# Expert weights loaded partition-major, and eight slab places instead of six in layer 1

## The chip, the cores and the metric

One core of a Trainium2 chip runs the whole program. The metric is device time in microseconds (us) from launch to end, lower is better. The engines are PE (TensorE), DVE (VectorE), ACT (ScalarE), POOL (GpSimd) and SP (SyncE); SP issues nearly all weight loads. The core has 16 DMA engines. Two times are to be held apart: the device time of a run, and the span of the one profiled execution, which counts from its first instruction to its last.

## What is computed

A backbone of two layers over 256 context and 256 latent tokens of width 1024, all in float32. Each layer mixes tokens (neighbourhood attention and a bidirectional recurrence) and then passes them through 16 experts, of which each token uses two of one group. Layer 1 needs the latent tokens only. The part that matters here:

```python
def grouped_moe(h, w_router, router_bias, w_gate, w_up, w_down):
    t = h.reshape(-1, shp[-1])
    scores = jax.nn.sigmoid((t @ w_router).astype(jnp.float32))
    ...
    out = jnp.zeros_like(t)
    for e in range(N_EXPERTS):
        h_e = jax.nn.silu(t @ w_gate[e]) * (t @ w_up[e])
        out = out + combine[:, e:e + 1] * (h_e @ w_down[e])
    return out.reshape(shp)
```

`w_gate[e]` and `w_up[e]` are 1024 x 512, `w_down[e]` is 512 x 1024: each is 2 MiB, and an expert has three. In the products t @ w_gate[e] the sum runs over 1024 features, in h_e @ w_down[e] over 512. A sum may be taken in any order of its terms, as long as both factors use the same.

## The kernel before

**Slabs.** Each 2 MiB weight matrix is one slab of 16 KiB in each of 128 partitions. PE sums over partitions, so a slab holds k blocks: 8 for gate and up, 4 for down. The load (`flat`, L1483) is written `(k p) n -> p k n`: partition p gets rows p, p + 128, p + 256 and so on. In memory these are single rows of 512 float32 (2 KB) for gate and up, of 1024 float32 (4 KB) for down. The left factors have the matching order: feature 128 k + p of a token stands in partition p of block k.

**Layer 0** (`dealt_experts`). 512 tokens. After the second norm the tokens are turned into rows (L1020), ACT copies them out of PSUM into `hrow` (L1988) and stores them as a table in memory; the copies of the first tile stand ahead of the sigmoid of the router scores (L1982) in ACT's order. For each expert POOL gathers its 128 rows (`feed_rows`, L2298), PE turns them back (L1066), and every product is made from high and low halves: weights are split by ACT (`high`, L2015) and DVE (`slab_lo`, L2872), then the matmuls of L1077, L1080 and L1086 (gate and up) and L1105, L1110 and L1115 (down) run. Between them DVE multiplies the up product with `f_silu` into `f_acts` (L2894), and PE turns that (L1094). Six slabs are in flight, two places for each kind (`LANE`). The expert's output is stored in `expert_table` and gathered after the last expert.

**Layer 1** (`narrow_experts(2)`). 256 tokens, up to 64 for each expert. The rows stay in SBUF as `hrow_hi` (ACT, L2001) and `hrow_lo` (DVE, L2848); selection matrices (L3011) pick an expert group's tokens by matmul (`gather_cols`, L1308). Then for each expert e:

- `into_hidden`: 16 matmuls, gate (L1328) into partitions 0 to 63 and up (L1329) into 64 to 127 of one bank. They need the gate and the up slab.
- ACT makes `gated` (L2170), DVE multiplies it with the up product into `hidden` (L3036).
- meanwhile PE runs `gather_cols` for one quarter of the next group (L1308, not for e of 12 and above) and, at even e, the scatter of the pair before (L1361).
- `turn_hidden` (L1339), ACT's copy, `down` (L1350, 8 matmuls for each half) with the down slab.

**Where slabs go in layer 1.** Slabs are numbered m = 3 e + kind. Slab m goes to place m % 6: the four ring places, a fifth (A0 + 92 KB), and a sixth over `hT`. SP issues in order, each load behind one wait (L1513). The first four wait for the ring places, which the last matrices of the layer (`in` 8 to 11, `out`) held; the fifth for the last norm (`h_ready`), the sixth for `hrow_lo` (`hrow_ready`). Slab m from 6 on waits until slab m - 6 is spent: `hidden_done` for gate and up, `halves_done` for down. The loads of the layer before that, the `("in", l, s)` and `("out", l, s)` matrices, go through the same queue and the four ring places (`fill`, L1473).

```python
w = (A["w_gate"], A["w_up"], A["w_down"])
flat = [x.rearrange("l e (k p) n -> (l e) p k n", p=P) for x in w]
...
for m in range(LANES):
    if m < SLOTS:
        sp.wait_ge(*slot_spent[last_in(base + m)])
    elif m == SLOTS:
        sp.wait_ge(sem["h_ready"], 4 * KT)
    else:
        sp.wait_ge(sem["hrow_ready"], 4)
    fill_expert(m, l * N_EXPERTS + m // 3)
```

Of the kernel before, what the change touches and what calls it, by code (L numbers as in the profile page):

```python
# [65 lines left out]
def build(nc, A, out, stop=99):  # L66
# [7 lines left out]
    def fixed(name, shape, dtype=f32, offset=None):  # L74
# [129 lines left out]
    hrow_lo = fixed("hrow_lo", [P, 4, D], f32r, offset=A0 + 16 * KB)  # L204
    y_hi = fixed("y_hi", [P, 2, D], f32r, offset=A0 + 32 * KB)
# [16 lines left out]
    pick4 = fixed("pick4", [P, 4, 4 * 64], f32r, offset=A0 + 48 * KB)  # L222
    pickw4 = fixed("pickw4", [P, 4, 4 * 64], offset=A0 + 52 * KB)
    gated = fixed("gated", [P, FF], offset=A0 + 56 * KB)
    hidden = fixed("hidden", [P, FF], offset=A0 + 58 * KB)
    hiddenT = fixed("hiddenT", [P, 4, 64], offset=A0 + 60 * KB)
    spread4 = fixed("spread4", [P, 2, 2, SEG], offset=A0 + 64 * KB)
    y_pair = fixed("y_pair", [P, 2, D], offset=A0 + 68 * KB)
    y_rows = fixed("y_rows", [P, 2, D], offset=A0 + 76 * KB)

    rt = [[fixed(f"rt{l}_{i}", [P, 4, N_GROUPS, PER_GROUP], offset=A0 + (40, 84)[l] * KB + 256 * i) for i in range(12)]
          for l in range(DEPTH)]
    scores_t = [fixed(f"scores_t{l}", [P, TOK], offset=A0 + (34, 88)[l] * KB) for l in range(DEPTH)]
# [10 lines left out]
    narrow_slab = [fixed(f"narrow_slab{i}", [P, SLOT], offset=(slab_at[:5] + [hT_at])[i]) for i in range(LANES)]  # L244
# [28 lines left out]
    names = """const_loaded vec_loaded x_loaded tables_loaded bias_loaded out_stored psum_ready side_ready cond_zeroed cond_ready  # L273
        pick2_ready ada_row ada_mod
        epsv_ready lower_ready square_ready square_added norm_std normed_ready h_ready q_ready
# [13 lines left out]
        dve_chain act_chain pool_chain""".split()  # L289
    with ExitStack() as ctx:  # L290
        sem = {n: ctx.enter_context(nc.semaphore(n)) for n in names}
        slot_full = [ctx.enter_context(nc.semaphore(f"slot_full{i}")) for i in range(LANES)]
# [13 lines left out]
        for l in range(DEPTH):  # L306
# [13 lines left out]
            for ph, n in ((2 * l, N_EXPERTS), (2 * l + 1, 3 * N_EXPERTS)):  # L320
                if ph == 1:

                    loads += [("ahead", i) for i in range(SLOTS)]
                    lane += range(SLOTS)
                keys = [("moe", ph, e, k) for e in range(n) for k in range(3)]
                loads += keys
                lane += [LANE[k][e % 2] if ph == 0 else n % (SLOTS, LANES)[l] for n, (_, _, e, k) in enumerate(keys)]
# [8 lines left out]
        def loads_before(ph):  # L337

            b = slot_of(("moe", ph, 0, 0))
            counts = [lane[:b].count(i) for i in range(LANES)]  # L340
            assert len(set(counts[:SLOTS])) == 1
            return counts
# [209 lines left out]
        def std_of(l, h):  # L552
            return ors_more[:, h - 2, :] if l == 0 and h >= 2 else ors[:, h % 2, :]

# [6 lines left out]
        def _(pe):  # L561
# [122 lines left out]
            for l in range(DEPTH):  # L684
# [606 lines left out]
                def narrow_experts(ph):  # L1291
# [3 lines left out]
                    def weights(i, e, g):  # L1295

                        m = 3 * e + g
                        full_at = 16 * (filled[m % LANES] + m // LANES + 1)
                        pe.wait_ge(slot_full[m % LANES], full_at if i is None else i * 32 + full_at)
                        return narrow_slab[m % LANES][:].rearrange("p (k n) -> p k n", k=(KT, KT, 4)[g])  # L1300

                    def gather_cols(i, e, b):

                        pe.wait_ge(*total(ph, i, "group_picked", e - e % 4 + 3, 1))
                        for k in range(2):
                            d = 2 * (e % 4) + k
                            for n, (t, rows) in enumerate([(t, rows) for t in tiles for rows in (hrow_hi, hrow_lo)]):
                                mm = T.matmul(bank[b][:, k * SEG:(k + 1) * SEG], rows[:, t, d * P:(d + 1) * P],  # L1308
# [148 lines left out]
        def _(sp):  # L1457
# [17 lines left out]

            for n in range(SLOTS):
# [4 lines left out]
            for l in range(DEPTH):  # L1481
# [5 lines left out]
                while n < base:  # L1487
                    if last_in(n) not in slot_spent:
                        break
                    if loads[n] == ada_loads[(6, 22)[l]]:  # L1490

                        sp.wait_ge(*is_ready(("o", l, HG_HEADS - 1)))
                        for r in range(4):
                            src = A["rel_bias_reversed"]
                            for h in range(NA_HEADS):
# [3 lines left out]
                                             .rearrange("p (a c) -> p a c", a=4), skew).then_inc(sem["bias_loaded"], 16)  # L1499
                    sp.wait_ge(*slot_spent[last_in(n)])  # L1500
# [4 lines left out]
                w = (A["w_gate"], A["w_up"], A["w_down"])  # L1505
                flat = [x.rearrange("l e (k p) n -> (l e) p k n", p=P) for x in w]
# [53 lines left out]
                else:  # L1560
                    for m in range(LANES):
                        if m < SLOTS:
                            sp.wait_ge(*slot_spent[last_in(base + m)])
                        elif m == SLOTS:
                            sp.wait_ge(sem["h_ready"], 4 * KT)
                        else:

                            sp.wait_ge(sem["hrow_ready"], 4)
                        fill_expert(m, l * N_EXPERTS + m // 3)
                    with sp.Fori(0, N_EXPERTS // 4 - 1) as i:  # L1570
                        for m in range(LANES, LANES + 12):
                            fill_spent(2 * l, i, 0, m)
                            fill_expert(m, i * 4 + (l * N_EXPERTS + m // 3))
                    for m in range(LANES + 36, 48):
                        fill_spent(2 * l, None, 0, m)
                        fill_expert(m, l * N_EXPERTS + m // 3)
# [39 lines left out]
        def _(act):  # L1616
            chained = [0]

            def link(ins):

                chained[0] += 1
                ins.then_inc(sem["act_chain"], 1)
                act.wait_ge(sem["act_chain"], chained[0])

            act.wait_ge(sem["vec_loaded"], 16)
            act.wait_ge(sem["cond_zeroed"], 1)
# [13 lines left out]
            def norm(key, count, lo, tail, ahead=None):  # L1640

                act.wait_ge(sem["epsv_ready"], 1)
# [1542 lines left out]
```

## Time and profile before

| | |
|---|---|
| device time, median of 3 runs | 1593.22 us (1591.72 to 1593.62) |
| device time of the profiled execution | 1591.69 us |
| its span | 1589.9 us, mean granted PE clock 0.959 |
| PE busy | 1436.4 us, 90% of the span |
| DVE busy | 854.5 us, 54% |
| ACT busy | 650.4 us, 41% |
| moved by DMA | 352.14 MB, mean 221 GB/s |
| experts of layer 0 | from the gather at 586 us to 887 us |
| experts of layer 1 | from 1314 us to 1569 us |

The views are read as follows. A **window** gives the busy time of each engine in a stretch, the granted PE clock (1.00 is 2.4 GHz), the mean busy share of the DMA engines and the rate that they moved. The **chain of waits** follows back from the last instruction what released each step; "issue" is time in which the engine waited for nothing that the profile shows, which for a matmul that needs a slab is the time until it has landed. The **timeline** lists instructions in order, with the idle time of the engine before them in brackets. The list of **waits** sums who waited for whom. The **groups** give the mean duration of instructions of one line and form.

### The profile page before, as it was taken

The numbers are of one execution on the slowest core, as the hardware profiler recorded it, in microseconds if no ns is written. First come the engines' busy times: TensorE is split into PE (matmuls) and PEld (weight loads), VectorE is DVE, ScalarE is ACT, GpSimd is POOL, SyncE is SP. The second block draws the span as 40 slices with busy tenths as digits, with TensorE's granted clock in tenths as the row PEclk, the third lists the DMA queues.
The fourth block names the chain that finished last, engine by engine and source line by source line (L and its number), as shares of the span: only waits on it lengthen the run. The fifth ranks groups of instructions, "written<-read, shape, count | busy, mean of one in ns | idle before, by whom it ended". The sixth has DMA issues, their size and how long they took to land.

```text
span 1589.9 us, 17079 instructions
## 1 busy us (share of the span) xinstructions
PE 1436.4 (90%) x6678; PEld 1006.1 (63%) x6678; DVE 854.5 (54%) x1112; ACT 650.4 (41%) x891; POOL 245.4 (15%) x210
## 2 busy tenths in 40 slices
PE   3999999989999869999999689999889978998884
PEld 0786667547888647888888478765568854433332
DVE  3477973865644448888888257870850141111003
ACT  2654443345323257887777265430340122111112
POOL 0007951400000011111120200750500000000000
PEclk9999999999999969999999899999999988999998
DMA  9511107790142437999999861116444456999992
GB/s 357 216 53 53 54 24 210 284 383 1 54 159 90 175 133 280 399 399 399 401 401 401 297 224 53 54 53 159 156 163 143 141 192 254 393 395 393 395 393 77
DMA packets 167146, 352.14 MB, mean 221 GB/s; under 512 B 21776, under 2 KB 22928, under 8 KB 167056
## 3 DMA queue, kind: packets, MB, share of 16 engines
q1 hardware_dynamic: 162880, 335.72, 57.9%
q0 software_dynamic: 3456, 12.58, 2.2%
q10 hardware_dynamic: 720, 2.62, 0.4%
q8 instruction: 58, 0.95, 0.3%
q14 instruction: 32, 0.26, 0.1%
HBM read 339.38 MB, written 11.53 MB: 221 GB/s over the span
## 4 chain that ended last, share of the span: by engine, by line
PE 76%; DVE 7%; DMA 6%; POOL 4%; issue 3%; ACT 3%; SPq 0%; DVEq 0%; ACTq 0%; POOLq 0%
PE bank L1328 7%; PE bank L745 4%; PE bank L1350 4%; PE bank L1086 4%; PE bank L1080 4%; PE bank L1077 4%; PE bank L629 4%; DMA ring<-in_w_ada 3%; PE bank L664 2%; PE bank L1105 2%; PE bank L892 2%; DMA ring<-in_w_in 2%; PE bank L894 2%; PE bank L645 2%; PE bank L897 2%
## 5 line engine op out<-in xcount | busy, mean ns | idle before, releaser
L2872 DVE TENSOR_TENSOR slab_lo<-slab,high 128x4096 fp32r<-128x4096 f32 x48 | 211.9, 4419 | 9.7 <-ACT high L2015 9.1
L2015 ACT ACTIVATE high<-slab 128x4096 fp32r<-128x4096 f32 x48 | 174.3, 3635 | 31.2 <-DMA slab<-in_w_up 13.3
L1328 PE MATMUL bank<-narrow_slab,picked 128*64 128x512 f32 x256 | 116.1, 608 | 11.9 <-issue 11.6
L2298 POOL DMA_INDIRECT feed_rows<-token_table,slot_token x16 | 45.4, 2840 | 482.8 <-DVE slot_token L2812 289.9
L1329 PE MATMUL bank<-narrow_slab,picked 128*64 128x512 f32 x256 | 116.2, 609 | 0.0
L745 PE MATMUL bank<-hT,ring 128*128 128x512 f32 (+1 forms) x256 | 104.1, 546 | 0.0
L1328 PEld LDWEIGHTS bank<-narrow_slab,picked 128*64 128x64 f32 x256 | 35.3, 140 | 83.2 <-issue 82.8
L3036 DVE TENSOR_TENSOR hidden<-bank,gated 64x512 f32<-64x512 f32 x16 | 11.1, 694 | 120.7 <-ACT gated L2170 120.7
L1852 ACT ACTIVATE gsig<-bank 128x512 f32<-128x512 f32 (+1 forms) x32 | 15.7, 491 | 141.0 <-PE bank L629 71.3
L629 PE MATMUL bank<-hT,ring 128*128 128x256 f32 x320 | 72.6, 382 | 0.0
L2258 POOL TENSOR_TENSOR pair<-pf 128x512 f32<-128x512 f32 (+1 forms) x32 | 34.5, 1078 | 220.6 <-DVE pb L2496 214.4
L745 PEld LDWEIGHTS bank<-hT,ring 128*128 128x128 f32 x256 | 46.8, 194 | 33.1 <-issue 31.5
L1077 PE MATMUL bank<-high,feed_hi 128*128 128x512 f32 x256 | 66.5, 403 | 0.8 <-ACT feed_hi L2022 0.8
L629 PEld LDWEIGHTS bank<-hT,ring 128*128 128x128 f32 x320 | 61.6, 193 | 8.4
L1080 PE MATMUL bank<-high,feed_lo 128*128 128x512 f32 x256 | 63.6, 391 | 1.8 <-DVE feed_lo L2879 1.8
L1086 PE MATMUL bank<-slab_lo,feed_hi 128*128 128x512 f32 x256 | 65.0, 396 | 0.0
L1350 PE MATMUL bank<-narrow_slab,hiddenT 128*64 128x512 f32 x256 | 58.5, 597 | 6.8 <-issue 6.8
L602 PE MATMUL bank<-ring,cond 128*32 128x512 f32 x384 | 51.8, 672 | 11.5 <-DMA ring<-in_w_ada 7.4
L769 PEld LDWEIGHTS bank<-pair 128*128 128x128 f32 x384 | 47.8, 193 | 22.3 <-DVE pair L2533 14.5
L2170 ACT ACTIVATE gated<-bank 64x512 f32<-64x512 f32 x16 | 9.4, 589 | 116.4 <-PE bank L1329 116.4
L769 PE MATMUL bank<-pair 128*128 128x128 f32 x384 | 49.3, 279 | 7.4 <-DVE pair L2533 7.4
L1080 PEld LDWEIGHTS bank<-high,feed_lo 128*128 128x128 f32 x256 | 48.2, 188 | 12.2 <-DVE feed_lo L2879 2.2
(356 smaller groups left out, 3040.6 us busy)
## 6 DMA issues: line engine op xcount, KB each, us to landing
ring<-in_w_ada SPq DMA_DIRECT2D x24, 2048.0 KB, 13.8
ring<-in_w_in SPq DMA_DIRECT2D x24, 2048.0 KB, 9.1
slab<-in_w_gate SPq DMA_DIRECT2D x16, 2048.0 KB, 15.5
slab<-in_w_up SPq DMA_DIRECT2D x16, 2048.0 KB, 14.8
slab<-in_w_down SPq DMA_DIRECT2D x16, 2048.0 KB, 14.5
narrow_slab<-in_w_gate SPq DMA_DIRECT2D x16, 2048.0 KB, 17.5
narrow_slab<-in_w_up SPq DMA_DIRECT2D x16, 2048.0 KB, 22.1
narrow_slab<-in_w_down SPq DMA_DIRECT2D x16, 2048.0 KB, 19.2
```

The costliest lines, as they stand in the source:

```text
L602: mm = T.matmul(o[r:r + 32, :], cond[:, k, a:a + 32], w[:, k, :], start=(n == first and k < 4), stop=(n + 1 == end and k >= 4))
L629: mm = T.matmul(o[:, lo:TOK], w[:, k, c * P:(c + 1) * P], hT[:, k, lo:TOK], start=(k == 0), stop=(k == KT - 1))
L745: mm = T.matmul(beside[0][:, a:TOK], w[:, k, c * P:(c + 1) * P], hT[:, k, a:TOK], start=(k == 0), stop=(k == KT - 1))
L769: mm = T.matmul(o[:, (2 * i + b) * P:(2 * i + b + 1) * P], left, right, start=True, stop=True)
L1077: T.matmul(bank[kind][:, :], feed_hi[e % 2][:, k, :], w[:, k, :], start=(k == 0), stop=False)
L1080: T.matmul(bank[kind][:, :], feed_lo[e % 2][:, k, :], w[:, k, :], start=False, stop=False)
L1086: mm = T.matmul(bank[kind][:, :], feed_hi[e % 2][:, k, :], w[:, k, :], start=False, stop=(k == KT - 1))
L1328: T.matmul(bank[0][0:64, :], x, gate[:, k, :], start=(k == 0), stop=(k == KT - 1))
L1329: mm = T.matmul(bank[0][64:128, :], x, up[:, k, :], start=(k == 0), stop=(k == KT - 1))
L1350: mm = T.matmul(bank[3][64 * half:64 * half + 64, :], hiddenT[:, k, :], w[:, k, half * 512:(half + 1) * 512], start=(k == 0), stop=(k == 3))
L2015: S.activation(half_of(e, kind)[:], w[:], ACT.Copy)\
L2872: V.tensor_tensor(low[:], w[:], half_of(e, kind)[:].bitcast(f32), ALU.subtract)\
```

## The change

1. The three expert tensors are loaded as `(p k) n -> p k n` in both layers: partition p gets the k rows that follow each other, 8 rows of 2 KB or 4 of 4 KB, 16 KB in one piece.
2. To match, the left factors are dealt in the same order when they are copied out of PSUM. `in_turn` reads every k-th element, `dealt` writes blocks: the token rows of layer 0 (`hrow`) and layer 1 (`last_hi`, `last_lo`, formerly `hrow_hi`, `hrow_lo`), and the hidden values `f_acts`, `acts` and `hidden`. Instructions and sizes stay; rows are read with a stride of 8 elements, hidden values with one of 4.
3. Layer 1 has eight places: the four of the ring, B0, `hT`, A0 + 16 KB and B0 + 16 KB. The order of the first round is `FIRST`: slabs 0 and 1 go to the two new places (6 and 7), slabs 2 to 5 to the ring, 6 to B0, 7 to `hT`.
4. Slabs 0 and 1 are issued ahead of the load `("in", 1, 10)`, behind a wait for `og_ready`, the last normed head of layer 1. Slab 6 waits for the last output product, slab 7 for the last turned rows.
5. SP's loop over layer 1's slabs becomes straight code with the same kind of waits. Small tiles (`pick4`, `gated`, `hidden`, `y_pair` and others) move, and the semaphores `cond_zeroed` and `epsv_ready` become one, `blanks_ready`.

```diff
@@ tiles of layer 1
+    last_hi = fixed("last_hi", [P, 2, D], f32r, offset=A0)
+    last_lo = fixed("last_lo", [P, 2, D], f32r, offset=A0 + 8 * KB)
...
-    narrow_slab = [fixed(f"narrow_slab{i}", [P, SLOT], offset=(slab_at[:5] + [hT_at])[i]) for i in range(LANES)]
+    FIRST, AGAIN = (6, 7, 0, 1, 2, 3, 4, 5), tuple(range(LANES))
+    narrow_at = slab_at[:SLOTS] + [B0, hT_at, A0 + 16 * KB, B0 + 16 * KB]
+    narrow_slab = [fixed(f"narrow_slab{i}", [P, SLOT], offset=narrow_at[i]) for i in range(len(FIRST))]
@@ new functions
+        def dealt(x, k, half=None):
+            y = x.rearrange("p (k c) -> p k c", k=k)
+            return y if half is None else y[:, :, half * P // 2:(half + 1) * P // 2]
+        def in_turn(x, k):
+            return x.rearrange("p (c k) -> p k c", k=k)
@@ SP
+            flat = [A[w].rearrange("l e (p k) n -> (l e) p k n", p=P) for w in ("w_gate", "w_up", "w_down")]
+            def fill_first(m):
+                at = FIRST[m % len(FIRST)]
+                sp.dma_start(narrow_slab[at][:].rearrange("p (k n) -> p k n", k=(KT, KT, 4)[m % 3]), flat[m % 3][N_EXPERTS + m // 3])\
+                    .then_inc(slot_full[at], 16)
...
+                    if loads[n] == ("in", 1, 10):
+                        sp.wait_ge(sem["og_ready"], 8)
+                        for m in range(2):
+                            fill_first(m)
                     sp.wait_ge(*slot_spent[last_in(n)])
                     fill(n)
...
-                flat = [x.rearrange("l e (k p) n -> (l e) p k n", p=P) for x in w]
...
+                    for m in range(2, 3 * N_EXPERTS):
+                        at = FIRST[m % len(FIRST)]
+                        if m >= len(FIRST):
+                            name, k = spent_by[l][(m - len(FIRST)) % 3]
+                            sp.wait_ge(*total(2, None, name, (m - len(FIRST)) // 3, k))
+                        elif at < SLOTS:
+                            sp.wait_ge(*slot_spent[last_in(base + m)])
+                        elif at == SLOTS:
+                            sp.wait_ge(*is_ready(("out", 1, KT - 1)))
+                        else:
+                            sp.wait_ge(*is_ready(("rows", 1, 3, 1)))
+                        fill_first(m)
@@ ACT
-                        S.activation(hrow[:, t, half * 512:(half + 1) * 512], result(("rows", l, t, half))[:, :],
+                        S.activation(dealt(hrow[:, t, :], KT, half), in_turn(result(("rows", l, t, half))[:, :], KT),
                                      ACT.Copy).then_inc(sem["rows_kept"], 1)
...
-                        S.activation(hrow_hi[:, t, half * 512:(half + 1) * 512], result(("rows", l, t, half))[:, :],
+                        S.activation(dealt(last_hi[:, t - 2, :], KT, half), in_turn(result(("rows", l, t, half))[:, :], KT),
                                      ACT.Copy).then_inc(sem["hrow_hi_ready"], 1)
@@ DVE
+                            V.tensor_tensor(dealt(last_lo[:, t - 2, :], KT, half), in_turn(result(("rows", l, t, half))[:, :], KT),
+                                            dealt(last_hi[:, t - 2, :].bitcast(f32), KT, half), ALU.subtract).then_inc(sem["hrow_ready"], 1)
...
-                        V.tensor_tensor(f_acts[:], bank[1][:, :], f_silu[:], ALU.mult).then_inc(sem["act_made"], 1)
+                        V.tensor_tensor(dealt(f_acts[:], 4), in_turn(bank[1][:, :], 4), in_turn(f_silu[:], 4), ALU.mult).then_inc(sem["act_made"], 1)
...
-                        V.tensor_tensor(hidden[64:128, :], bank[0][64:128, :], gated[64:128, :], ALU.mult)                         .then_inc(sem["hidden_ready"], 1)
+                        V.tensor_tensor(dealt(hidden[64:128, :], 4), in_turn(bank[0][64:128, :], 4), in_turn(gated[64:128, :], 4), ALU.mult)                         .then_inc(sem["hidden_ready"], 1)
```

## Rows read from the trace of the kernel before

**Rows 1.** Windows: PE PEld DVE ACT POOL busy; PEclk, DMA share, GB/s.
```profile
1320.00:1330.00 10.00, 9.75 (x53) 4.67 (x52) 2.30 (x4) 3.07 (x4) 0.00 (x0) 0.98 0.00 0
...
1340.00:1550.00 210.00, 190.31 (x858) 79.31 (x856) 23.58 (x34) 27.84 (x52) 0.00 (x0) 0.98 1.04 394
```

**Rows 2.** Chain of waits, layer 1's experts: start us, us, what.
```profile
1373.24 3.65 PE bank L1350 x16
...
1383.76 1.15 PE bank L1308 x8
...
1389.26 3.65 PE bank L1350 x16
...
1402.17 3.65 PE bank L1350 x16
...
1405.82 2.28 issue
...
1551.74 0.61 PE bank L1328
```

**Rows 3.** Chain of waits, layer 0's experts.
```profile
636.11 1.81 PE bank L1105 x8
...
653.80 1.81 PE bank L1105 x8
...
867.59 1.81 PE bank L1105 x8
```

**Rows 4.** Timeline of SP, layer 1: start us, us, engine line op.
```profile
1154.12 1.44 SPq L1473 DMA_DIRECT2D ring<-in_w_hg_o  x1
...
1198.89 22.82 SPq L1473 DMA_DIRECT2D ring<-in_w_in  x2
...
1312.40 0.37 SPq L1513 DMA_DIRECT2D narrow_slab<-in_w_down  x1
```

**Rows 5.** Timeline of DVE, the last normed head of layer 1.
```profile
1186.89 0.48 DVE L2690 SCALAR_TENSOR_TENSOR oh<-oh,vec,hgate 128x256 f32<-128x256 f32 x1
```

**Rows 6.** Windows in which one length of row passes.
```profile
1347.00:1357.00 10.00, 10.00 (x49) 4.47 (x46) 1.39 (x2) 1.77 (x3) 0.00 (x0) 1.00 1.05 387
...
1357.50:1362.50 5.00, 5.00 (x23) 2.10 (x23) 0.69 (x1) 0.38 (x1) 0.00 (x0) 1.00 1.03 409
...
1293.50:1297.50 4.00, 0.49 (x2) 0.09 (x2) 2.60 (x4) 1.19 (x3) 0.00 (x0) 0.87 0.97 351
...
8.00:10.00 2.00, 0.00 (x0) 0.00 (x0) 0.00 (x0) 0.21 (x1) 0.00 (x0) 1.00 1.04 418
```

**Rows 7.** DMA queues: packets, MB, share of 16 engines.
```profile
q1 hardware_dynamic: 162880, 335.72, 57.9%
```

**Rows 8.** DVE groups by form: shapes xcount | busy us, mean ns | idle.
```profile
L2364 DVE TENSOR_TENSOR mod<-bank,vec 128x32 f32<-128x32 f32 x5 | 0.9, 188 | 5.9 <-PE bank L614 5.9
...
L2761 DVE TENSOR_TENSOR rt<-rt,rt 128x32 f32<-128x32 f32 x2 | 0.4, 192 | 0.1
...
L2761 DVE TENSOR_TENSOR rt<-rt,rt 128x64 f32<-128x64 f32 x2 | 0.5, 225 | 0.1
...
L2353 DVE TENSOR_REDUCE pick_expert<-const 128x16 f32<-128x64 f32 x1 | 0.2, 246 | 0.0
...
L2760 DVE TENSOR_REDUCE rt<-rt 128x16 f32<-128x64 f32 x2 | 0.4, 222 | 0.1
```

**Rows 9.** Chain of waits, routing of layer 1.
```profile
1303.36 1.10 ACT hrow_hi L2001 x2
...
1309.89 2.48 DVE hrow_lo L2848 x4
```

**Rows 10.** Waits of PE, 1310 to 1590: us in total, times, longest.
```profile
PE bank L1339 <- DVE hidden L3036: 4.7, 9, 1.4
```

**Rows 11.** Timeline of DVE, one expert of layer 0; waits of POOL to 620.
```profile
701.05 0.69 DVE L2894 TENSOR_TENSOR f_acts<-bank,f_silu 128x512 f32<-128x512 f32 x1 [2.05 <-issue]
...
POOL feed_rows L2298 <- DVE slot_token L2812: 289.9, 1, 289.9
```

More of the change, by code:

```diff
@@ L221, in build @@
     picked = fixed("picked", [P, 2, KT, 4 * 64], offset=A0 + 32 * KB)
[L222 to L231, printed above, removed]
+    pick4 = fixed("pick4", [P, 4, 4 * 64], f32r, offset=B0 + 32 * KB)
+    pickw4 = fixed("pickw4", [P, 4, 4 * 64], offset=B0 + 36 * KB)
+    gated = fixed("gated", [P, FF], offset=B0 + 40 * KB)
+    hidden = fixed("hidden", [P, FF], offset=B0 + 42 * KB)
+    hiddenT = fixed("hiddenT", [P, 4, 64], offset=B0 + 44 * KB)
+    spread4 = fixed("spread4", [P, 2, 2, SEG], offset=B0 + 48 * KB)
+    y_pair = fixed("y_pair", [P, 2, D], offset=B0 + 52 * KB)
+    y_rows = fixed("y_rows", [P, 2, D], offset=A0 + 40 * KB)
+    rt = [[fixed(f"rt{l}_{i}", [P, 4, N_GROUPS, PER_GROUP], offset=A0 + (40 * KB, 93 * KB + 64)[l] + 256 * i) for i in range(12)]
           for l in range(DEPTH)]
-    scores_t = [fixed(f"scores_t{l}", [P, TOK], offset=A0 + (34, 88)[l] * KB) for l in range(DEPTH)]
+    scores_t = [fixed(f"scores_t{l}", [P, TOK], offset=(A0 + 34 * KB, B0 + 40 * KB)[l]) for l in range(DEPTH)]
     assert A0 + 102 * KB <= END
@@ L288, in build @@
         chunk_high chunk_low row_over way_high way_low tile_high tile_low head_high head_low
-        dve_chain act_chain pool_chain""".split()
+        dve_chain pool_chain""".split()
     with ExitStack() as ctx:
         sem = {n: ctx.enter_context(nc.semaphore(n)) for n in names}
-        slot_full = [ctx.enter_context(nc.semaphore(f"slot_full{i}")) for i in range(LANES)]
+        slot_full = [ctx.enter_context(nc.semaphore(f"slot_full{i}")) for i in range(len(FIRST))]
         bank = [ctx.enter_context(nc.psum_tensor(f"bank{i}", [P, 512], f32)) for i in range(8)]
@@ L327, in build @@
                 loads += keys
-                lane += [LANE[k][e % 2] if ph == 0 else n % (SLOTS, LANES)[l] for n, (_, _, e, k) in enumerate(keys)]
+                turn = (None, tuple(range(SLOTS)), FIRST, AGAIN)[ph]
+                lane += [LANE[k][e % 2] if ph == 0 else turn[n % len(turn)] for n, (_, _, e, k) in enumerate(keys)]
         def slot(key):
@@ L339, in loads_before @@
             b = slot_of(("moe", ph, 0, 0))
-            counts = [lane[:b].count(i) for i in range(LANES)]
+            counts = [lane[:b].count(i) for i in range(len(FIRST))]
             assert len(set(counts[:SLOTS])) == 1
@@ L1297, in weights @@
                         m = 3 * e + g
-                        full_at = 16 * (filled[m % LANES] + m // LANES + 1)
-                        pe.wait_ge(slot_full[m % LANES], full_at if i is None else i * 32 + full_at)
-                        return narrow_slab[m % LANES][:].rearrange("p (k n) -> p k n", k=(KT, KT, 4)[g])
+                        turn = FIRST if ph == 2 else AGAIN
+                        at = turn[m % len(turn)]
+                        full_at = 16 * (filled[at] + m // len(turn) + 1)
+                        pe.wait_ge(slot_full[at], full_at if i is None else i * 32 + full_at)
+                        return narrow_slab[at][:].rearrange("p (k n) -> p k n", k=(KT, KT, 4)[g])
                     def gather_cols(i, e, b):
@@ L1306, in gather_cols @@
                             d = 2 * (e % 4) + k
-                            for n, (t, rows) in enumerate([(t, rows) for t in tiles for rows in (hrow_hi, hrow_lo)]):
-                                mm = T.matmul(bank[b][:, k * SEG:(k + 1) * SEG], rows[:, t, d * P:(d + 1) * P],
+                            for n, (t, rows) in enumerate([(t, rows) for t in tiles for rows in (last_hi, last_lo)]):
+                                mm = T.matmul(bank[b][:, k * SEG:(k + 1) * SEG], rows[:, t - 2, d * P:(d + 1) * P],
                                               pick4[:, t, :], start=(n == 0), stop=(n == 2 * len(tiles) - 1))
@@ L2970, in expert @@
                         dve.wait_ge(*total(ph, i, "act_turned", e - 1, 1))
-                        V.scalar_tensor_tensor(acts[:], bank[1][:, :], slot_weight[:, e % 2:e % 2 + 1], silu[:],
+                        V.scalar_tensor_tensor(dealt(acts[:], 4), in_turn(bank[1][:, :], 4), slot_weight[:, e % 2:e % 2 + 1],
+                                               in_turn(silu[:], 4),
                                                ALU.mult, ALU.mult).then_inc(sem["act_ready"], 1)
```

34 lines of the change are left out of this document (6 added, 28 removed).

## Prediction

> **What bounds the kernel now.** I read the windows of layer 1's experts first, then the chain of waits there, SP's queue, and layer 0's experts. The windows [rows 1] show DMA moving nothing while PE starts the experts at 1320 us, and then 394 GB/s without a gap from 1340 to 1550 us: from the first refill on, these experts live on a stream that runs full. The chain of waits shows from when this costs. While weights are there, two experts take 28.93 us (down products of every second expert at 1373.24 and 1402.17), and PE sets the pace. At 1405.82 stands the first "issue", 2.28 us ahead of the gate product of expert 6, whose slab had not landed. The last expert's gate product starts at 1551.74 [rows 2]. Had PE set the pace throughout: expert 5's gate product started at 1389.26 + 3.65 = 1392.91; five pairs later it is 1537.6; experts 12 and 14 have no next group to gather (1.15 us each, as at 1383.76 [rows 2]), so 1535.3. The stream costs 1551.7 - 1535.3 = 16.4 us.
>
> Layer 0's experts are bounded by PE. Down products of experts 1 and 2 start at 636.11 and 653.80, a period of 17.69 us; that of expert 14 starts at 867.59, where 653.80 + 12 x 17.69 = 866.1 was due [rows 3]. The stream costs 1.5 us there, late.
>
> **Two more places.** Six slabs are there before the first expert frees one; now eight. SP's queue [rows 4] shows the room: between the fill at 1154.12 and that at 1198.89 it issues nothing. The change puts two fills ahead of the latter, behind the wait for the last normed head, whose instruction ends at 1187.37 [rows 5]. This wait ends 11.5 us before the fill queued behind it may go, and two slabs need 10.8 us at 387 GB/s, so even the transfers are over by then. Cost 0; if that head came after 1198, each us of it would pass to the fill. Slabs 2 to 5 take the four ring places under the waits that slabs 0 to 3 have now. Slab 6 follows when the output projection has been read, slab 7 when the rows have been turned; now SP waits until 1312.40 for its sixth [rows 4], which the DVE differences hold back. Both kernels refill first when expert 0's gate and up product is over, near 1329.
>
> At today's rate a slab takes 2.097 MB / 394 GB/s = 5.32 us, and the last up slab (number 46) lands two slabs sooner: the last expert starts at 1551.7 - 10.6 = 1541.1, still after PE's 1535.3. The places alone give 10.6 us.
>
> **One row of 16 KB for each partition.** Gate and up slabs now come in rows of 2 KB, down slabs in rows of 4 KB. In the full stream the two can be told apart: 387 GB/s while 2 KB rows pass, 409 while 4 KB rows do [rows 6]. A slab takes 5.42 or 5.13 us: 32 packets fewer on each of 16 DMA engines save 0.29 us. From 32 to 8 packets the same slope saves 0.22 more: 4.9 us, 428 GB/s. Bounds: 5.13 if only the rate of 4 KB rows is reached, 5.32 if nothing changes, more if long rows are read worse (a rival). That rows which join in memory are moved as one is borne out by a count: q1's 162880 packets [rows 7] are just 117 slabs of 1024, 36 of 512, 1920 for the stores of y, 1024 for the output, 16384 for the bias, 1408 for the tables and 16 for each of 244 transfers, if the mask table's 14 joining rows of 512 B went as one of 7168 B; cut, they would add 1664.
>
> PE is the bound once a slab takes less than (1535.3 - 1333.6) / 39 = 5.17 us, where 1333.6 = 1551.7 - 41 x 5.32 is the refills' start with their landing and 39 slabs remain. Even 5.13 passes. So layer 1 gains the whole 16.4 us; late next is PE. In layer 0 the lateness of 1.5 us goes: an expert moves 6.29 MB of weights and 1.05 MB of rows, 7.34 MB in 17.69 us = 415 GB/s, and 428 suffices.
>
> SP's loop becomes straight code with the same waits in the same order, the merged semaphores are waited for once at the start, and the moved tiles follow the same readers: cost 0, since none of it is queued ahead of other work.
>
> **Deals in eviction.** Rows and hidden values are now read with a stride of 32 or 16 B out of PSUM, same counts and sizes. VectorE reading 32 elements of PSUM in pairs 32 B apart took 188 ns, a plain one in SBUF 192: no cost. VectorE reading single elements 128 B apart took 246 ns for 64, a plain one 222: 0.375 ns an element, 0.19 us for 512 [rows 8]. I take 0.15 us an instruction, from 0 to 0.2, nearer to the second row because single elements are what is read here; no row has ScalarE with a stride, it gets the same value. On the path lie:
> - layer 1: two ScalarE copies (1.10 us, the sigmoid of the scores is behind them) and four VectorE differences (2.48 us, the places are behind them) [rows 9]: 6;
> - layer 1: the hidden product. PE waits for it at 9 of 16 experts [rows 10]; at the others the scatter covers it: 9;
> - layer 0: two copies before the scores, and expert 15's product: 3. The other products are covered, VectorE idling 2.05 us before each [rows 11]; without that cover 0.15 us each. The other six copies are covered too: the gather waits for VectorE's slot numbers, not for the tokens [rows 11].
>
> Together 18 x 0.15 = 2.7 us.
>
> **Sum.** 16.4 + 1.5 - 2.7 = 15.2 us less. The profiled execution took 1591.7 us (span 1589.9 and 1.8 around it), so 1576.5; it lay 1.5 below the median of the three runs, 1593.2, so 1578.0.
>
> **Rivals.**
> *The stream keeps its rate* (rows are cut again, or something else than packets holds it). For it: nothing in the trace shows that the gain from 2 to 4 KB goes on to 16. Against: the two rates of rows 6, of which even the second suffices. The places give 10.6 us, the deals take 1.4 (6 instructions in layer 1 and 3 in layer 0; those in the experts vanish under DMA): 1593.2 - 9.2 = 1584.0.
>
> *A stride takes a second cycle for each element.* 32 elements more cost 33 ns (192 to 225 [rows 8]), so 512 at two cycles cost 0.53 us more, 18 of them 9.5 us: 1593.2 - 17.9 + 9.5 = 1584.8. For it: nowhere does this trace read 512 single elements at a stride out of PSUM. Against: the pairs at 188 ns. The Trainium skill, Advanced Engine Details and Errata (Memory Cachelines), speaks for this rival: PSUM has lines of two FP32 values, SBUF of four, and each access to a new line is penalised. By it the pairs are just the harmless case and every dealt read the harmful one; it names no price.
>
> *Slower: long rows are read at a lower rate.* The partitions' streams start 16 KB apart instead of side by side. Each per cent of rate lost costs 39 x 0.053 = 2.1 us in layer 1 and, for some 14 experts, 14 x 0.18 = 2.6 us in layer 0. It eats the 9.2 us of the places at 2% less, near 386 GB/s in the mean. At 351 GB/s, the rate of a lone slab's window [rows 6], 11% less, it costs 52 us: 1593.2 - 9.2 + 52 = 1636. For it: no row has this pitch. 
>
> **How the numbers follow.** Forecast 0.64; rate kept 0.13; strides dear 0.13; long rows slow 0.06; unnamed 0.04, half of it faster. The range: strides at no cost and a store after layer 0 that lands sooner on an emptier queue (2 us) give 1593.2 - 19.9 = 1573.3; the two fast rivals end at 1584.8. So 1572.5 to 1585.5. A measurement can't tell less than 0.2% (3.2 us) from no change; only rates near the slow rival's turning point give that, 0.03. Faster 0.91, slower 0.06.
>
> **What would show it.** Above 405 GB/s through layer 1's experts, and "issue" gone ahead of gate products. Two experts every 29 us to the end. The hidden product at 0.85 us. Layer 0's down products 17.7 us apart to the last. Two fills in SP's queue at 1187. The prediction is wrong if the rate stays below 405 GB/s or the hidden product takes over 1 us.

## The result

The changed kernel takes 1578.61 us (median of 4 runs, 1574.67 to 1581.51) where the kernel before took 1593.2 beside it (1591.72 to 1593.62): a ratio of 0.9907 with a 95% interval of 0.9887 to 0.9926, 14.6 us less. Forecast were 1578.0, 15.2 us less. The profiled execution took 1578.95 us (span 1577.1), only 12.7 us less than that of before; where the rest of the 15.2 went is the matter of the sections below.

Line numbers of the changed kernel, where rows name them: gate and up products L1345 and L1346, the turn of hidden L1356, down products L1367, the gather L1325, `hidden` L3052, `f_acts` L2909, `last_hi` L2017, `last_lo` L2863; layer 0's down products begin with L1120; SP fills the ring at L1490 and layer 1's slabs at L1498.

**The stream.** Windows of layer 1's experts in the changed kernel, columns as in [rows 1] (here and in later blocks, "..." stands for lines left out):

```profile
1340.00:1500.00 160.00, 151.94 (x717) 65.14 (x712) 24.39 (x29) 23.80 (x44) 0.00 (x0) 1.00 1.01 428
...
1530.00:1540.00 10.00, 9.48 (x40) 3.85 (x38) 1.75 (x2) 1.56 (x3) 0.00 (x0) 1.00 0.00 0
```

428 GB/s where [rows 1] have 394, and by 1530 the stream is over: it ends ahead of the experts instead of setting their end. The queue of the loads says why:

```profile
q1 hardware_dynamic: 93248, 335.72, 55.4%
```

Against 162880 in [rows 7] these are 69632 packets fewer for the same bytes. 64 gate and up slabs that go from 1024 to 128 packets and 32 down slabs that go from 512 to 128 make 57344 + 12288 = 69632. So each partition's 16 KB now travel as one packet.

**The places.** SP's timeline in the changed kernel:

```profile
1188.90 0.34 SPq L1498 DMA_DIRECT2D narrow_slab<-in_w_gate  x1
1189.29 0.43 SPq L1498 DMA_DIRECT2D narrow_slab<-in_w_up  x1
1199.00 22.82 SPq L1490 DMA_DIRECT2D ring<-in_w_in  x2
...
1304.66 0.33 SPq L1498 DMA_DIRECT2D narrow_slab<-in_w_up  x1
1327.62 0.33 SPq L1498 DMA_DIRECT2D narrow_slab<-in_w_down  x1
```

The two new fills stand where [rows 4] show a hole, and the fill behind them still goes at 1199.00 (1198.89 before). The eighth slab is issued at 1304.66, where the sixth went at 1312.40.

**The experts.** Waits of PE between 1310 and 1590 in the changed kernel (us in total, times, longest):

```profile
PE bank L1356 <- DVE hidden L3052: 8.1, 9, 1.8
PE bank L1367 <- issue: 6.8, 13, 0.5
```

No wait for a slab ahead of a gate product is left. The 6.8 us ahead of the down products stood in the kernel before too, 13 times, 0.5 us each: there PE waits for ACT's copy of the turned hidden values, not for a slab. The kernel before, in the same view:

```profile
PE bank L1328 <- issue: 11.6, 6, 2.9
```

In its place the wait for `hidden` has grown from 4.7 us [rows 10] to 8.1. The groups of VectorE and ScalarE in the changed kernel, by form, show which instructions paid for the deals and which did not:

```profile
L3052 DVE TENSOR_TENSOR hidden<-bank,gated 64x512 f32<-64x512 f32 x16 | 17.2, 1075 | 104.4 <-ACT gated L2186 104.4
...
L2909 DVE TENSOR_TENSOR f_acts<-bank,f_silu 128x512 f32<-128x512 f32 x16 | 17.4, 1088 | 26.1 <-issue 26.1
...
L2863 DVE TENSOR_TENSOR last_lo<-bank,last_hi 128x512 fp32r<-128x512 f32 x4 | 2.5, 682 | 0.0
...
L2017 ACT ACTIVATE last_hi<-bank 128x512 fp32r<-128x512 f32 x4 | 2.2, 595 | 0.1
...
L2004 ACT ACTIVATE hrow<-bank 128x512 f32<-128x512 f32 x8 | 4.1, 609 | 0.3 <-PE bank L1035 0.3
```

`hidden` took 694 ns before and takes 1075, `f_acts` 691 and 1088. The other three, which read PSUM with a stride of 32 B, took 682, 596 and 610 ns before and take the same now (682, 595 and 609).

**Where the profiled 12.8 us of span come from**, by the start of the same step in both chains of waits:

| stretch | before to after, us |
|---|---|
| up to layer 0's first down product (618.40, 619.20) | +0.8, ahead of all that the change touches in the experts |
| layer 0's experts 0 to 14 (to 867.59, 866.94) | -1.45: the lateness is gone |
| layer 0's expert 15 (to its last eviction, 886.46, 887.78) | +0.4 for `f_acts`, +1.6 for products at a lower clock |
| to layer 1's first pick (1313.87, 1313.43) | -1.75, of it 0.6 in the store of layer 0's last rows (5.24 and 4.61) |
| the gather (6.64, 5.64) | -1.0: the same 32 products at a granted clock of 0.56 before, 0.69 after |
| first to last gate product (1321.92 to 1551.74, 1320.49 to 1538.77) | -11.5 |
| from there to the end | +0.2 |

The stages in which the change moves nothing of PE's work, ahead of the experts, between the layers and in the gather, thus differ by up to 1.8 us. The 1.0 of the gather is no gain of the change: the same kernel once more (e0) takes 6.69 us for these products.

### The profile page after: what moved, and what is told of

It is laid out like the page before. It is cut to its first block, busy times and chain, and to the rows that moved or that the text cites. A ratio compares the mean times of both kernels' runs of the same rounds, so it can differ in the third digit from the quotient of the medians.

```text
span 1577.1 us, 17012 instructions
## 1 busy us (share of the span) xinstructions
PE 1431.3 (91%) x6678; PEld 1003.1 (64%) x6678; DVE 864.6 (55%) x1112; ACT 652.1 (41%) x891; POOL 245.0 (16%) x210
## 3 DMA queue, kind: packets, MB, share of 16 engines
q1 hardware_dynamic: 93248, 335.72, 55.4%
## 4 chain that ended last, share of the span: by engine, by line
PE 76%; DVE 9%; DMA 6%; POOL 3%; ACT 3%; issue 2%; SPq 0%; DVEq 0%; ACTq 0%; POOLq 0%
PE bank L1345 7%; PE bank L760 4%; PE bank L1367 4%; PE bank L1095 4%; PE bank L1092 4%; PE bank L644 4%; PE bank L1101 3%; DMA ring<-in_w_ada 3%; PE bank L679 2%; DMA ring<-in_w_in 2%; PE bank L1120 2%; PE bank L907 2%; PE bank L909 2%; PE bank L1125 2%; PE bank L660 2%
## 5 line engine op out<-in xcount | busy, mean ns | idle before, releaser
L1345 PE MATMUL bank<-narrow_slab,picked 128*64 128x512 f32 x256 | 112.5, 592 | 0.2 <-ACT picked L2210 0.2
L1346 PE MATMUL bank<-narrow_slab,picked 128*64 128x512 f32 x256 | 112.5, 592 | 0.0
L1345 PEld LDWEIGHTS bank<-narrow_slab,picked 128*64 128x64 f32 x256 | 35.0, 137 | 67.3 <-issue 66.8
L3052 DVE TENSOR_TENSOR hidden<-bank,gated 64x512 f32<-64x512 f32 x16 | 17.2, 1075 | 104.4 <-ACT gated L2186 104.4
L1367 PE MATMUL bank<-narrow_slab,hiddenT 128*64 128x512 f32 x256 | 60.2, 612 | 6.8 <-issue 6.8
L3058 DVE COPY y_pair<-bank 64x512 f32<-64x512 f32 x16 | 11.1, 694 | 80.6 <-PE bank L1367 80.6
## 6 DMA issues: line engine op xcount, KB each, us to landing
narrow_slab<-in_w_down SPq DMA_DIRECT2D x16, 2048.0 KB, 10.5
```

The source lines that it names most:

```text
L1345: T.matmul(bank[0][0:64, :], x, gate[:, k, :], start=(k == 0), stop=(k == KT - 1))
L1346: mm = T.matmul(bank[0][64:128, :], x, up[:, k, :], start=(k == 0), stop=(k == KT - 1))
L1367: mm = T.matmul(bank[3][64 * half:64 * half + 64, :], hiddenT[:, k, :], w[:, k, half * 512:(half + 1) * 512], start=(k == 0), stop=(k == 3))
```

## The experiments

Theory: rows of 16 KB end layer 1's dependence on the stream, the places only soften it, and the deals cost what the strided operand in SBUF costs. The rivals stand in the expectations. e0 to e3 ran on one chip, beside 11 runs of the kernel before with a median of 1591.96 us; e7, e5, e6 and e4 on another, beside 11 runs with 1593.21. Medians of e0, e1, e2, e3, e7 and e5 are of 6 runs, that of e6 of 4, e4 is one run. Differences in us are between medians; the intervals of the ratios are 0.002 to 0.0026 wide to either side, 3 to 4 us, so a difference of 2 us between two of these kernels isn't settled by their times.

### The changed kernel once more (e0)

> The changed kernel again, beside its parts on one chip. 1578.6 us, within 3. If the hidden product's length is what the change pays, it is 1.07 us again for each of 16 (0.69 in the kernel before).

Measured: 1576.82 us (1575.61 to 1580.18), 0.9897 (0.9872 to 0.9921) of before. The base for the three that follow.

### The places alone (e1)

```diff
-            flat = [A[w].rearrange("l e (p k) n -> (l e) p k n", p=P) for w in ("w_gate", "w_up", "w_down")]
+            flat = [A[w].rearrange("l e (k p) n -> (l e) p k n", p=P) for w in ("w_gate", "w_up", "w_down")]
@@ dealt and in_turn return plain blocks
```

> The eight places and the early fills alone; weights in rows of 2 and 4 KB as before, nothing dealt. My theory (the stream's rate bounds layer 1's experts, and two more slabs are a head start of two slab times): 394 GB/s as before, the last gate product 10.6 us earlier, 1582.6 us; the hidden product at 0.69 us. Rival (the places only move the wait, as slabs are spent at PE's pace): within 2 us of 1593.2.

Measured: 1582.45 us (1578.72 to 1585.1), 0.9923 (0.9898 to 0.9948). The first window and the first wait of its profile:

```profile
1340.00:1500.00 160.00, 153.37 (x722) 65.71 (x720) 20.12 (x29) 23.79 (x44) 0.00 (x0) 1.00 1.04 394
```

```profile
PE bank L1346 <- issue: 4.9, 4, 2.8
```

The rate is that of before and PE still waits for slabs (here L1346 is the gate product), 4 times instead of 6 and 4.9 us instead of 11.6. The two places alone gave 9.5 us between the medians, and the interval of the ratio holds from 8 to 16 us. The traces are sharper: from the issue of the first refill to the last gate product the kernel before takes 222.5 us (1329.20 to 1551.74), e1 212.1 (1331.27 to 1543.35). That is 10.5 us less, where two slab times had promised 10.6.

### The rows alone (e2)

The kernel before, its six places and its order of loads, with the partition-major load and the dealt evictions:

```diff
-                flat = [x.rearrange("l e (k p) n -> (l e) p k n", p=P) for x in w]
+                flat = [x.rearrange("l e (p k) n -> (l e) p k n", p=P) for x in w]
@@ and the evictions with dealt and in_turn, as in the change
```

> The rows of 16 KB and the deals alone, with the six places and the waits of the kernel before. My theory (one bound at a time): at 427 GB/s a slab takes 4.91 us, the last gate product could start at 1332.2 + 41 x 4.91 = 1533.5 us, before PE gets to it at 1538.8, so the six places suffice and the time is that of the changed kernel, 1578.6 us within 2; no issue ahead of gate products. Rival (the two parts add up, each taking its share of the stream's 16.4 us): the rows alone give what the places don't, 5.8 us, less 3.8 for the deals: about 1590 us.

Measured: 1578.67 us (1578.04 to 1580.51), 0.9907 (0.9884 to 0.9931), with no wait for a slab ahead of a gate product, and this window:

```profile
1340.00:1500.00 160.00, 152.02 (x714) 65.47 (x714) 24.22 (x29) 23.98 (x45) 0.00 (x0) 1.00 1.01 428
```

13.3 us from the rows alone and 9.5 from the places alone make 22.8, where both together gave 15.1: each removes the same wait. The prediction's own working had this in it, unsaid: its turning point of 5.17 us a slab holds for eight places, where 39 slabs remain. With six, 41 remain, and it is (1535.3 - 1333.6) / 41 = 4.92, which 4.90 passes too, but only just.

### Deals by ScalarE (e3, e7)

ScalarE deals its result as it leaves PSUM; VectorE reads that in runs and only PSUM with the stride:

```diff
-                        S.activation(gated[64:128, :], bank[0][0:64, :], ACT.Silu).then_inc(sem["gated"], 1)
+                        S.activation(dealt(gated[64:128, :], 4), in_turn(bank[0][0:64, :], 4), ACT.Silu).then_inc(sem["gated"], 1)
...
-                        V.tensor_tensor(dealt(hidden[64:128, :], 4), in_turn(bank[0][64:128, :], 4), in_turn(gated[64:128, :], 4), ALU.mult)                         .then_inc(sem["hidden_ready"], 1)
+                        V.tensor_tensor(dealt(hidden[64:128, :], 4), in_turn(bank[0][64:128, :], 4), dealt(gated[64:128, :], 4), ALU.mult)                         .then_inc(sem["hidden_ready"], 1)
@@ the same for f_silu and f_acts, silu and acts
```

> The changed kernel, but ScalarE deals the silu of the gate product while it copies it out of PSUM, so that VectorE reads only the up product with a stride, and its SBUF operand in runs. Theory A (the stride on SBUF costs, the one on PSUM nothing): the hidden product and layer 0's product back from 1.08 to 0.69 us, ScalarE's silu stays at 0.59; 9 or 10 products on the path, 3.8 us less than the changed kernel: 1574.8 us. Theory B (the stride of 16 B on PSUM costs, where 32 B did not): products stay at 1.08 and ScalarE's silu goes to 0.98 too, on the path at 10 experts: 1582.5 us. Theory C (two strided operands together cost, each alone nothing): as A.

> The kernel after with the deals of the hidden values made by ScalarE (the kernel of e3) once more, as the base for the two runs beside it. If the gain of 2.1 us over the kernel after was real and not scatter, it takes 1574.7 again (1573.5 to 1576), against 1576.8 for the kernel after beside the same kernel before; if it was scatter, 1576.5 to 1578. Hidden product 0.69 us, f_acts 0.69 us, a pair of layer 1's experts 28.9 us.

Measured: e3 1574.69 us (1572.76 to 1578.06), 0.988 (0.9856 to 0.9905); e7, the same kernel, 1576.45 (1573.23 to 1576.78), 0.989 (0.9869 to 0.9911). The groups of e7:

```profile
L3052 DVE TENSOR_TENSOR hidden<-bank,gated 64x512 f32<-64x512 f32 x16 | 11.1, 695 | 104.4 <-ACT gated L2186 104.4
L2909 DVE TENSOR_TENSOR f_acts<-bank,f_silu 128x512 f32<-128x512 f32 x16 | 11.1, 691 | 30.5 <-issue 28.2 <-PE bank L1101 2.4
...
L2186 ACT ACTIVATE gated<-bank 64x512 f32<-64x512 f32 x16 | 9.4, 589 | 100.0 <-PE bank L1346 100.0
```

```profile
PE bank L1356 <- DVE hidden L3052: 4.7, 9, 1.4
```

With the stride on PSUM only, both products take what they took before, ScalarE's Silu with a stride of 16 B takes 589 ns, and PE's wait is back at 4.7 us. In time, e3 lay 2.1 us under e0 beside the same kernel before, where 3.8 were forecast; e7 missed its 1574.7 and stands between the ranges that its expectation gave to a real gain and to scatter, but lies 16.8 us below its own before, as e3 does by 17.3, and the changed kernel by 14.6 and 15.1. The intervals of the ratios overlap, so time alone doesn't settle these 2 us. The traces agree with them: from the first to the last `hidden`, e0 takes 216.35 us (1326.40 to 1542.75) with the clock full at each down product between them, e7 215.13 (1327.66 to 1542.79), of which 1.7 are a down product at a lower clock (below), so 213.4 without. The 2.9 between are the 8 such waits of this stretch by 0.37. Of this gain some is given back in layer 0: from its first down product to that of expert 14 the four executions with ScalarE's deals (e3, e7, e5, e6) take 248.2 to 248.3 us, the four others with rows of 16 KB 247.7; why isn't known. This kernel has the lowest median on either chip, though not clear of the scatter of the others with long rows.

### Rows and ScalarE's deals with six places (e5)

e2 with e3's edits.

> Rows of 16 KB with the deals made by ScalarE, but the six old places and no early fills: the only difference to the kernel of e3 are the places. Theory: once a slab takes 4.9 us the places are worth nothing, because the last up slab is the 41st refill and lands near 1328.5 + 41 x 4.9 = 1529 us, ahead of the 1535 at which PE can first want it: 1575 us, within 1.5 of the kernel of e3, and no issue ahead of gate products. Rival: with the cheaper hidden product PE takes six slabs in 28.92 us, 4.82 each, a little faster than the stream brings them (4.90), so six places run dry somewhere between experts 2 and 15 and the two more places are worth 2 us or more: 1577 or above, with issue ahead of gate or down products.

Measured: 1576.87 us (1570.72 to 1578.07), 0.9891 (0.9868 to 0.9915), beside e7's 1576.45. No wait for a slab ahead of a gate product. Its time alone doesn't decide against the rival, which forecast 1577 or above; the missing wait does. Windows and PE's timeline of e5:

```profile
1534.00:1536.00 2.00, 2.00 (x12) 0.86 (x10) 0.00 (x0) 0.00 (x0) 0.00 (x0) 1.00 0.96 410
1536.00:1538.00 2.00, 2.00 (x12) 0.78 (x10) 0.69 (x1) 0.59 (x1) 0.00 (x0) 1.00 0.27 115
1538.00:1540.00 2.00, 2.00 (x12) 0.77 (x10) 0.00 (x0) 0.00 (x0) 0.00 (x0) 1.00 0.00 0
```

```profile
1515.99 5.34 PE L1359 MATMUL bank<-narrow_slab,hiddenT 128*64 128x512 f32 x16 [0.52 <-issue]
...
1536.19 0.59 PE L1337 MATMUL bank<-narrow_slab,picked 128*64 128x512 f32 x1
```

The stream ends at 1536.5 (115 of 428 GB/s in the last two us) with a down slab; the up slab before it had been moved one slab time, 4.9 us, sooner, at 1531.6. A product can't start at once. The end of the stream and the last gate product of the kernel before show by how much:

```profile
1554.00:1556.00 2.00, 2.00 (x12) 0.77 (x10) 0.00 (x0) 0.00 (x0) 0.00 (x0) 1.00 0.48 197
```

```profile
1551.74 0.61 PE L1328 MATMUL bank<-narrow_slab,picked 128*64 128x512 f32 x1 [0.65 <-issue]
```

There the stream ends near 1555.0, the up slab had been moved a down slab's 5.13 us sooner, at 1549.8, and the product that waited for it starts 1.9 us later (1.8 by the same reckoning in e1). So in e5 the slab was ready near 1533.5, an estimate, and the last gate product starts at 1536.19: 2.7 us to spare. Of these, 1.7 come from the down product at 1515.99, which ran at a lower clock (5.34 us instead of 3.65, see below); without it 1.0 is left. So six places suffice, but narrowly: at 16 KB a row the two more places are worth nothing that can be measured, and the theory held. The expectation had the slab there at 1529, more than 4 us too soon: it counted from the issue of the first refill as if slabs were ready without delay.

### Rows of 8 KB (e6)

e3 with each 16 KB loaded in two pieces, from the tensor's two halves:

```diff
-            flat = [A[w].rearrange("l e (p k) n -> (l e) p k n", p=P) for w in ("w_gate", "w_up", "w_down")]
+            flat = [A[w].rearrange("l e (h p k) n -> (l e) p h k n", h=2, p=P) for w in ("w_gate", "w_up", "w_down")]
```

> The kernel of e3 with each partition's 16 KB loaded as two rows of 8 KB from two places 1 MiB apart (gate and up: 4 rows of 2 KB that follow each other, down: 2 of 4 KB); the deals stay those of 16 KB rows, so the blocks of the weights don't match their left factors. It measures the rate at a length of row that neither kernel has. Theory (a packet costs the same at every length): 16 packets an engine for each slab where 16 KB rows need 8, 0.07 us more, 4.98 us a slab, 421 GB/s in layer 1's stream, 96 x 128 = 12288 packets more in the queue of the loads than the kernel after, and no longer time, since 4.98 is under the 5.17 from which PE waits: 1574.7, as e3. Rival (16 KB rows read well because one piece of memory is read in order, not because of their packets): the rate stays near that of 4 KB rows, 409 GB/s, 5.13 us a slab, 1574.7 to 1576.

Measured: 1577.56 us (1575.14 to 1580.02), 0.9899 (0.9873 to 0.9925) of before, and from its windows and its queues:

```profile
1340.00:1500.00 160.00, 154.13 (x726) 66.17 (x724) 20.12 (x29) 23.79 (x44) 0.00 (x0) 1.00 1.01 421
```

```profile
q1 hardware_dynamic: 105536, 335.72, 55.7%
```

421 GB/s was forecast by the cost of a packet, and 93248 + 12288 = 105536 is the count. So the gain of long rows fits a fixed cost for each packet: 387 GB/s at 2 KB and 409 at 4 KB [rows 6], 421 at 8 KB and 428 at 16 KB. In slab times, 5.42, 5.13, 4.98 and 4.90 us for 64, 32, 16 and 8 packets an engine: each packet less saves 9 or 10 ns, from end to end. The rival (409) falls: with 8 KB no partition's 16 KB are one piece of memory, and the rate still rises. The time is 2.9 us above the 1574.7 forecast, 1.1 above e7's, within their scatter.

### Which stride costs (e4)

```diff
-                        V.tensor_tensor(dealt(f_acts[:], 4), in_turn(bank[1][:, :], 4), in_turn(f_silu[:], 4), ALU.mult).then_inc(sem["act_made"], 1)
+                        V.tensor_tensor(dealt(f_acts[:], 4), dealt(bank[1][:, :], 4), in_turn(f_silu[:], 4), ALU.mult).then_inc(sem["act_made"], 1)
...
-                        V.tensor_tensor(dealt(hidden[64:128, :], 4), in_turn(bank[0][64:128, :], 4), in_turn(gated[64:128, :], 4), ALU.mult)                         .then_inc(sem["hidden_ready"], 1)
+                        V.tensor_tensor(hidden[64:128, :].rearrange("p (k c) -> p c k", k=4), bank[0][64:128, :].rearrange("p (c k) -> p c k", k=4), gated[64:128, :].rearrange("p (c k) -> p c k", k=4), ALU.mult)                         .then_inc(sem["hidden_ready"], 1)
```

> Prices two forms, in the kernel after. Layer 0: f_acts is made with the up product read from PSUM without a stride and silu from SBUF with the stride of 16 B, so the two are no longer of the same column. Layer 1: hidden is made from both operands without a stride and written with a stride of 512 B. Theory A (the SBUF operand's stride alone costs): f_acts 1.08 us. Theory C (only two strided operands together cost): f_acts 0.69 us. For the write: if each new line in SBUF costs on the way out as on the way in, hidden takes 1.08 us or more; if writes are free of it, 0.69. Where the deal is put decides nothing else, so the time is that of the kernel after, 1576.8, less 0 to 3 us.

Measured, in one run of 1578.02 us:

```profile
L2909 DVE TENSOR_TENSOR f_acts<-bank,f_silu 128x512 f32<-128x512 f32 x16 | 17.4, 1086 | 26.2 <-issue 26.2
L3052 DVE TENSOR_TENSOR hidden<-bank,gated 64x512 f32<-64x512 f32 x16 | 16.9, 1055 | 104.4 <-ACT gated L2186 104.4
```

The stride of 16 B on the SBUF operand alone costs all of it (1086 against 1088 with both strided), and a write to SBUF with a stride of 512 B costs nearly the same (1055). Theory A stands. With e3, where only PSUM is strided and nothing is lost, the price is settled: 0.36 to 0.40 us for 512 single elements of SBUF, none for those of PSUM.

## Why the prediction came out

**What bounds, and that it goes: right.** The 16.4 us of layer 1 were the stream's, they went whole, and PE was next, as forecast. From the first gate product (1321.92) to the forecast 1535.3 are 213.4 us at PE's pace. The changed kernel takes 218.3, of which 3.4 are the longer waits for `hidden` (8.1 instead of 4.7) and 1.7 a lower clock, told below; 213.2 are left. 428 GB/s were forecast and measured, by the step that was least sure, the slope of packet costs carried from 32 packets to 8; e6 bore it out at 16.

**The places: right alone, and covered by the rows.** 10.6 forecast; 9.5 between the medians and 10.5 in the trace measured (e1). The sum took them and the rows as one gain, which was right. It left open what the places add on top of the rows: 0.4 us (e5 beside e7) or 1.9 (e2 beside e0), both within the scatter of the runs.

**The deals: the term that was mis-sized.** 18 instructions by 0.15 us were forecast, 2.7 us. The six ScalarE and VectorE steps in layer 1's routing and the two copies in layer 0 cost nothing; the nine hidden products on the path and layer 0's last `f_acts` cost 0.38 and 0.40. That is 10 x 0.38 = 3.8 us instead of 2.7. The step that failed is the choice of the nearest row. The single elements of [rows 8] (`pick_expert` from `const`) are read from SBUF, and the forecast took them for PSUM too. What costs is single elements apart in SBUF, which only the products read (the differences read `last_hi` in runs of 64). There an element cost 0.74 ns (0.38 us / 512), twice the 0.375 of that row. I had written that the prediction is wrong if the hidden product takes over 1 us. It takes 1.08, so that term failed by its own test; the total moved by 1.1 us only, 2.3 too little on ten instructions and 1.2 too much on eight. That the two errors partly cancelled is luck.

**The second-cycle rival was half right.** Its 0.53 us an instruction did not come (0.38), and not at PSUM. The Trainium skill, Advanced Engine Details and Errata (Memory Cachelines), on which it drew, says that SBUF has lines of 16 bytes and wants at least two hits on one; the 1086 ns of e4 agree with that. Its words on PSUM, that every two consecutive elements should be contiguous, name matmuls as what slows down; the prediction took them for evictions. On VectorE and ScalarE no such loss is seen here: 682, 595 and 609 ns at 32 B, 695 and 589 at 16 B, all as without a stride.

**Layer 0: right, and eaten in the profiled execution.** Down products 17.69 us apart to that of expert 14; its 1.45 us came. Then expert 15 lost 1.6 us to the clock.

**What the sum did not have: the clock.** Between the last gate and up products of one expert and the down products, PE idles for `hidden` and for ACT's copy; when it starts again it is sometimes granted the lower of its two levels for a while. In the profiled execution of the changed kernel, its chain of waits and windows:

```profile
1505.10 3.65 PE bank L1367 x16
...
1518.36 5.35 PE bank L1367 x16
```

```profile
1516.00:1518.00 2.00, 0.46 (x4) 0.33 (x4) 1.05 (x1) 0.36 (x2) 0.00 (x0) 1.00 1.02 434
1518.00:1520.00 2.00, 1.64 (x6) 0.70 (x8) 0.00 (x0) 0.26 (x1) 0.00 (x0) 0.78 1.02 434
1520.00:1522.00 2.00, 2.00 (x8) 0.67 (x6) 0.00 (x0) 0.00 (x0) 0.00 (x0) 0.50 0.99 414
1522.00:1524.00 2.00, 2.00 (x12) 0.80 (x10) 0.25 (x1) 0.25 (x1) 0.00 (x0) 0.87 1.01 418
```

0.50 is 1.2 GHz, and the 16 down products take 5.35 us instead of 3.65: 1.7 us. The same step of e0, the same kernel with the same idle times ahead of it, in its timeline of PE:

```profile
1515.53 0.46 PE L1356 MATMUL bank<-const,hidden 64*128 64x64 f32 x4 [1.76 <-DVE hidden L3052]
1516.51 3.65 PE L1367 MATMUL bank<-narrow_slab,hiddenT 128*64 128x512 f32 x16 [0.52 <-issue]
```

Expert 15's down product, the last, has the same wait ahead of it, and there it is e0 that falls, while the changed kernel takes 3.65:

```profile
1544.83 5.35 PE L1367 MATMUL bank<-narrow_slab,hiddenT 128*64 128x512 f32 x16 [0.52 <-issue]
```

In layer 0's expert 15 the changed kernel was granted 0.60 from 880 to 884, where e0 and the kernel before had 1.00. These are the three places in the ten profiled executions, by PE's idle times just before them (1.75 instead of 1.76 in e4):

| place, idle us | lower level granted | full clock |
|---|---|---|
| layer 0, expert 15, 1.20 + 0.73 | changed kernel, e2, e4 | e0 |
| layer 0, expert 15, 0.84 + 0.73 | none | before, e1, e3, e5, e6, e7 |
| layer 1, expert 13, 1.76 + 0.52 | changed kernel, e2, e4 | e0 |
| layer 1, expert 13, 1.41 + 0.52 | e5, e6, e7 | before, e1, e3 |
| layer 1, expert 15, 1.76 + 0.52 | e0 | changed kernel, e2, e4 |
| layer 1, expert 15, 1.41 + 0.52 | e1, e3, e5, e6, e7 | before |

In layer 1 the clock falls or not after the same idle times, so it differs from one execution of a kernel to the next. Every profile but that of before, on which the forecast stands, has at least one fall there, 1.7 us each. In layer 0 it fell only after the longer wait, which the strided `f_acts` makes, in three profiles of four against none of six: its 1.6 us may be a further price of the stride. That is not shown, what decides is open, and no experiment was made on it.

**The gap, closed.** The profiled execution gained 12.7 us where 15.2 were forecast. The two falls of the clock (1.7 and 1.6), the deals (1.1) and the later start (0.8) take 5.2 us from the forecast; between the layers and in the gather 1.75 and 1.0 came that the sum did not have. 5.2 - 2.75 = 2.45 of the 2.5. Of the 1.75, 0.6 are the store of layer 0's last rows, which the prediction had in its range and not in its sum. From its issue to the first gather behind it, the kernel before and e1 take 6.06 and 6.79 us, the eight executions with longer rows 4.06 to 5.71; so these 0.6 go with the long rows, though no run isolates them. The gather is scatter (e0), and the other 1.1 are not explained. The profiled execution of e0 took 1577.02 us, 14.9 less than the median of its kernel before, with one fall of 1.7 us, at its last expert. The medians, 14.6 and 15.1 less, lie near the forecast, but the last us or two of this are luck: neither the falls of the clock nor what came between the layers stood in the sum, and runs of the changed kernel spread from 1574.67 to 1581.51.

## What to carry to other kernels

Where a stream of weights sets the end, count its packets first: rows that a partition reads in one piece (here 16 KB instead of 2 or 4) bought 9% of rate with no engine time, and more buffers for the same wait then bought nothing, so two remedies for one wait are tried apart before both are kept. A reordering that such a load demands goes into the eviction from PSUM, where it was free on both engines; as soon as single elements apart are read from or written to SBUF, VectorE took about half of the instruction more.

## What the runs showed of the hardware

- Rate of loads by length of row, one core: 387 GB/s at 2 KB, 409 at 4 KB, 421 at 8 KB, 428 at 16 KB; 9 to 10 ns a packet on each of 16 engines, if the difference is put down to their number. The Trainium skill, DMA: Bandwidth & Descriptors (Specifications), gives 435 GB/s as the ceiling of the fabric; 428, the most seen here over a longer stretch, agrees with it.
- VectorE, 512 float32 elements with single elements 16 B apart in SBUF: 1086 ns instead of 691; written 512 B apart: 1055. From PSUM at 16 or 32 B: no difference, nor on ScalarE.
- The granted clock fell to 1.2 GHz after idle times of 1.76 and 0.52 us in one execution and not in another of the same kernel, and likewise after 1.41 and 0.52 us (e7 and e3 at expert 13); the 16 down products then took 5.35 us instead of 3.65.
- A product that waited for a 2 MiB slab started 1.8 to 1.9 us after the slab's last bytes had been moved (before and e1, an estimate from windows of 2 us).
